# A two-layer attention and mixture-of-experts trunk: attention values of the small heads computed turned and in pairs, from probabilities divided early, and a router that takes its input by feature blocks

## The chip, the cores and the metric

The kernel runs on one core of one Trainium2 chip. The metric is the device time of one execution in microseconds; the time given for a kernel is the median of several runs. All arithmetic on the path is float32.

## The reference, cut to what matters

Two layers, each with a mixing part (three kinds of attention side by side) and a mixture of 32 experts with a router. Sequence 256, width 1024.

```python
for l in range(DEPTH):                              # 2 layers
    z = _rms_norm(x, norm_mix[l]) @ w_in[l]
    ya = _diff_attention(...)                       # "A": 4 heads of 128 value columns
    yb = _dsa_attention(...)                        # "B": 4 heads of 64
    yc = _mla(...)                                  # "C": 4 heads of 64
    mix = jnp.concatenate([ya, yb, yc], axis=-1)
    x = x + mix @ w_out[l]
    x = x + _hier_moe(_rms_norm(x, norm_ffn[l]), ...)
return _rms_norm(x, norm_final)

# in each attention, for 128 queries: p = softmax(logits); out = p @ v
# in _hier_moe: group and expert logits = normed x @ w_group, w_expert; 2 of the 8 experts
# of the best group per token; h = silu(x @ w_gate[e]) * (x @ w_up[e]); y = h @ w_down[e]
```

## The kernel before, in words

The program is written out by hand for each engine, with semaphores between them; each engine runs its own instructions in the order of the code. The 256 tokens lie in two tiles of 128 (`t` = 0, 1). The expert weights (32 experts in each layer, three chunks of 2 MB each: gate, up, down) stream through a ring of eight slots of 2 MB and three further places that hold other tensors during the attention part (two in `arena`, one made of `x` and `bias`). A load is issued by the queue on SP when its slot has been given back (`slot_free`), or when the tensor that lay in its place is no longer read. In the first round of a layer SP issues the chunks in the order `[0..5, 8, 9, 6, 7, 10, 12, 13, 11, 14, ...]`: 8 and 9 wait until the attention's last squares are summed (`ssq_ready`), 6 and 7 until an output matrix's slot is free, 10 for `sums_open` and `x_spent`, and 12 and 13 (`REFILL`) for the first products of expert 0 (`steps_used`). A quarter of chunk 11 goes to `spare`, the upper half of `xT`.

The attention part works through 16 steps (`STEPS`): four of kind C, four of kind B, eight of kind A; the first half of each kind is for tile 0 and the second for tile 1. A step of C or B covers two heads ("maps") side by side. For one step: `logits` (TensorE, two steps per call), `front` (VectorE: scale, bias, and the largest value), `exp` (ScalarE, which also sums the row), `combine` (VectorE: the reciprocal of the sum; for A also the difference of two maps), `turn_p` (TensorE transposes the probabilities), `turned` (ScalarE copies them to SBUF), `values` (TensorE), `finish` (VectorE divides the result by the sum and writes it to `rows`). Projections of the layer's input (`pair`, `columns`, `av_rows`) are put between these steps by hand as work for TensorE.

After the last steps the eight blocks of 128 mixed features of a tile are transposed (`turn_mix`), copied by ScalarE to `xT` (`mixT`) and multiplied by the output matrix (`out_half(t, half, k0, k1)`: blocks k0 to k1 for 512 output columns). `add_half` adds the result to `x`; `squares` and POOL give the RMS factor; `turn_xn` transposes `x` for the router, with a stride of 8 features, and `router(t)` multiplies it by 40 columns. `route` (VectorE) chooses the experts, `place_first` and `gather_first` bring the tokens to their experts, and `products` (at L1738) is the first work on expert weights. The next layer, or the end, follows after 32 experts.

Of the kernel before, what the change touches and what calls it, by code (L numbers as in the profile page):

```python
# [20 lines left out]
ALU = mybir.AluOpType  # L21
# [7 lines left out]
P = 128  # L29
# [54 lines left out]
PJ_EV = 9 + 4 + 2  # L84
# [143 lines left out]
def trunk(nc, x_d, w_in, w_out, norm_mix, norm_ffn, rel_bias, lam_q1, lam_k1, lam_q2, lam_k2,  # L228
          diff_subln, mla_q_norm, mla_kv_norm, w_uq, w_ukv, w_group, b_group, w_expert, b_expert,
          w_gate, w_up, w_down, norm_final, consts_d, onehot_d, flip_d, out_d):  # L230
# [3 lines left out]
    with ctx:  # L234
# [39 lines left out]
        ssq, mean, rms = sb("ssq", 16), sb("mean", 16), sb("rms", 16)  # L274
# [51 lines left out]

        spare = (xT[:, KD // 2:, :].rearrange("p j s -> p (j s)"),)
        h_rows = take(HALF)
        y = take(D_MODEL)
        pick = take(TOK * P).rearrange("p (t s) -> p t s", t=TOK)  # L330
# [66 lines left out]
        xnT_done, xnT_read, xnT_upper = sem("xnT_done"), sem("xnT_read"), sem("xnT_upper")  # L397
# [70 lines left out]
        def load_router(eng, l):  # L468

            loads = (  # L470
                (wr[:, :, 0:N_GROUPS], w_group.rearrange("l (p j) n -> l p j n", j=KD)[l]),
                (wr[:, :, R_EXP:], w_expert.rearrange("l (p j) n -> l p j n", j=KD)[l]),
                (br[:, 0:N_GROUPS], bcast_row(b_group, l, N_GROUPS)),
                (br[:, R_EXP:], bcast_row(b_expert, l, N_EXPERTS)),
            )
# [8 lines left out]
        def _(sp):  # L484
# [8 lines left out]
            for l in range(DEPTH):  # L493
# [24 lines left out]
                for m in range(ROUNDS):  # L518
# [18 lines left out]
                    for c in order_of(m):  # L537
# [49 lines left out]
                        if m == 0 and c == 7:  # L587
                            sp.wait_ge(router_done, at(l, TOK, TOK))
# [10 lines left out]
        def _(pool):  # L599
# [24 lines left out]
            for l in range(DEPTH):  # L624
# [16 lines left out]
                rms_of(own, base, 7, [(15, 16, D_MODEL)])  # L641
# [11 lines left out]
        def _(act):  # L653
# [16 lines left out]
            act.dma_start(gain_R, norm_ffn.rearrange("l (p j) -> p l j", j=KD)).then_inc(gain_r_in, 16)  # L670
# [13 lines left out]
            for l in range(DEPTH):  # L684
# [39 lines left out]
                def turned(s):  # L724
# [3 lines left out]
                    if s >= 2:  # L728
                        act.wait_ge(pv_done, at(l, PV_USES, 3 + s - 1))
                    copy(pT[:, s % 2, 0:n], src[:, 0:n]).then_inc(tr_read, 1)  # L730

                def mixT(t):
                    act.wait_ge(lam_ready, at(l, 2, 2))
                    for half in range(2):
                        if t == 0:
                            src, read = pj_wait(), pj_read
                        else:
                            act.wait_ge(mix_turned, at(l, 2, half + 1))
                            src, read = lg[:, half], mix_read
                        copy(xT[:, 4 * half:4 * half + 4, t * P:(t + 1) * P], src.rearrange("p (j s) -> p j s", j=4),  # L740
                             scale=gsub if half == 0 else 1.0).then_inc(read, 1)
# [62 lines left out]
                for t in range(TOK):  # L804
                    for half in range(TOK - t):
                        act.wait_ge(xnT_done, at(l, 4, 2 * t + half + 1))
                        copy(xT[:, 4 * half:4 * half + 4, t * P:(t + 1) * P],
                             (tr, pj)[t][:, half].rearrange("p (j s) -> p j s", j=4)).then_inc(xnT_read, 1)
# [99 lines left out]
        def _(dve):  # L908
# [11 lines left out]
            for l in range(DEPTH):  # L920
# [140 lines left out]
                def combine(s):  # L1061
# [5 lines left out]
                    if kind == "A":  # L1067
                        own.after()
# [5 lines left out]
                def finish(s):  # L1074

                    kind, i, t = STEPS[s]
                    dve.wait_ge(pv_done, at(l, PV_USES, 3 + s + 1))
                    src = pv[:, (3 + s) % 2, 0:P]
                    if kind == "A":
                        dst = rows[:, t, P * i:P * i + P]  # L1080
                    else:
                        o = {"B": 512, "C": 768}[kind]
                        dst = rows[:, t, o:o + 256].rearrange("p (m h d) -> p h m d", m=2, h=2)[:, i]
                    if kind == "A":
                        v.tensor_scalar(dst, src, rden[:, s % 4, 0:1], None, ALU.mult).then_inc(pv_read, 1)
                        dve.wait_ge(pv_read, at(l, PV_USES, 3 + s + 1))
                        col = 6 + 4 * t + i
                        own.after()
                        own.mark(v.tensor_tensor_reduce(out=sq, in0=dst, in1=dst, scale=1.0, scalar=0.0, op0=ALU.mult,
                                                        op1=ALU.add, accum_out=ssq[:, col:col + 1]))  # L1090
                    else:
                        v.tensor_tensor(dst, src.rearrange("p (m d) -> p m d", m=2),
                                        spread(rden[:, s % 4, :], 2, 64), ALU.mult).then_inc(pv_read, 1)
# [10 lines left out]
                front(2); front(3); combine(2); combine(3); finish(0); finish(1)  # L1104
# [4 lines left out]
                front(4); front(5); combine(4); combine(5); finish(2); finish(3)  # L1109
                front(6); front(7); combine(6); combine(7); finish(4); finish(5)  # L1110
                front(8); front(9); finish(6); finish(7); combine(8); combine(9)
# [11 lines left out]
                finish(14); finish(15)  # L1123
                own.after()
                dve.sem_inc(ssq_ready, 1)
# [20 lines left out]
                def squares(t):  # L1146

                    dve.wait_ge(x_added, at(l, 4, 2 * t + 2))
                    v.tensor_tensor_reduce(out=zT_flat[:, 0:D_MODEL], in0=x[:, t, :], in1=x[:, t, :],
# [794 lines left out]
```

## Time and profile before

| | |
|---|---|
| median of 3 runs | 1207.34 us (1206.68 to 1208.55) |
| the profiled execution | 1206.32 us, of which the profile's span is 1204.5 us |
| TensorE matmul busy (PE) | 1054.3 us, 88% of the span |
| VectorE (DVE) | 344.7 us, 29% |
| ScalarE (ACT) | 235.3 us, 20% |
| GpSimd (POOL) | 18.0 us, 1% |
| DMA | 446.00 MB, mean 370 GB/s |

The profile comes from one execution. Busy time of PE is modelled and includes the flow of data through the array, so that neighbouring matmuls overlap; what one costs is read from the distance between two starts. Each float32 matmul is recorded as two instructions ("x16" is eight matmuls); a transpose of 128x128 is one. PEld is the weight load that goes with a matmul. The span leaves out 1.8 us of the profiled execution.

### The profile page before, as it was taken

How to read it: one execution, taken by the hardware profiler on the slowest of the kernel's cores; microseconds unless marked ns; L12 is line 12 of the kernel's file. 1: busy time of each engine (PE TensorE's matmuls, PEld its weight loads, DVE VectorE, ACT ScalarE, POOL GpSimd, SP SyncE). 2: the span in 40 equal slices, each digit the busy share in tenths (PEclk: the TensorE clock that was granted, in tenths of full speed). 3: DMA queues.
4: the chain of work that ended last, by engine and by line, in shares of the span. 5: the costliest groups of instructions: out<-in, count | busy, mean ns of one | idle time of the engine just before them, and what ended most of it. 6: DMA issues, size and time to landing. Idle time of an engine off the chain costs nothing.

```text
span 1204.5 us, 18674 instructions
## 1 busy us (share of the span) xinstructions
PE 1054.3 (88%) x7889; PEld 594.6 (49%) x7892; DVE 344.7 (29%) x966; ACT 235.3 (20%) x578; POOL 18.0 (1%) x49
## 2 busy tenths in 40 slices
PE   9999999987887888778999999999887968787886
PEld 5777564443434343434468765554443434334433
DVE  3445563211111111111247365622111111111112
ACT  1234311111111111111112441121111111111112
POOL 1000100000000000000010000000000000000000
PEclk9999999998888889888999999999988988898899
DMA  8677579999999999999998056899999999999995
GB/s 303 218 278 280 227 271 429 426 427 426 426 428 424 429 425 427 426 427 427 414 389 309 26 221 254 318 426 428 426 426 426 428 425 427 425 425 427 425 429 214
DMA packets 59142, 446.00 MB, mean 370 GB/s; under 512 B 10888, under 2 KB 15536, under 8 KB 32176
## 3 DMA queue, kind: packets, MB, share of 16 engines
q1 hardware_dynamic: 57216, 443.57, 89.6%
q8 instruction: 65, 1.06, 0.4%
q10 hardware_dynamic: 1840, 1.19, 0.3%
q14 instruction: 21, 0.17, 0.0%
HBM read 442.63 MB, written 2.11 MB: 369 GB/s over the span
## 4 chain that ended last, share of the span: by engine, by line
PE 49%; DMA 44%; SPq 3%; DVE 2%; issue 1%; ACT 1%; POOL 0%; POOLq 0%; ACTq 0%; DVEq 0%
DMA ring<-in_w_up 39%; PE pv L1738 11%; PE pj L1396 8%; PE tr L1757 4%; PE pj L1637 4%; DMA arena<-in_w_up 4%; PE lg L1765 4%; PE pj L1765 3%; SPq L577 3%; PE pj L1402 2%; PE pj L1487 2%; PE tr L1725 1%; PE lg L1426 1%; PE pv L1749 1%; PE pj L1608 1%
## 5 line engine op out<-in xcount | busy, mean ns | idle before, releaser
L1738 PE MATMUL pv<-ring,xT 128*32 128x256 f32 x3136 | 287.7, 446 | 84.5 <-DMA ring<-in_w_up 52.2
L1738 PEld LDWEIGHTS pv<-ring,xT 128*32 128x32 f32 x3136 | 141.9, 123 | 188.2 <-issue 140.7
L1235 DVE TENSOR_SCALAR arena<-arena 128x128 f32<-128x128 f32 x64 | 14.5, 227 | 663.5 <-ACT arena L817 663.2
L1765 PE MATMUL lg<-arena 128*128 128x512 f32 x256 | 131.9, 597 | 0.0
L1765 PE MATMUL pj<-arena 128*128 128x512 f32 x256 | 130.7, 592 | 0.0
L656 ACT ACTIVATE arena<-pv 128x256 f32<-128x256 f32 x64 | 24.5, 383 | 512.2 <-PE pv L1738 512.2
L656 ACT ACTIVATE arena<-tr 128x512 f32<-128x512 f32 (+3 forms) x168 | 92.3, 558 | 125.1 <-PE tr L1757 107.0
L1738 PE MATMUL pv<-arena,xT 128*32 128x256 f32 x640 | 88.5, 434 | 19.6 <-DMA ring<-in_w_up 19.6
L1396 PE MATMUL pj<-xT,ring 128*128 128x256 f32 x448 | 100.6, 381 | 0.0
L1396 PEld LDWEIGHTS pj<-xT,ring 128*128 128x128 f32 x448 | 83.9, 190 | 12.9 <-issue 1.0
L1757 PE MATMUL tr<-ring,arena 128*32 128x512 f32 x696 | 84.2, 594 | 1.9 <-issue 1.9
L1765 PEld LDWEIGHTS pj<-arena 128*128 128x128 f32 x256 | 48.6, 190 | 61.2 <-issue 61.2
L1738 PEld LDWEIGHTS pv<-arena,xT 128*32 128x32 f32 x640 | 42.7, 120 | 47.6 <-issue 34.8
L1765 PEld LDWEIGHTS lg<-arena 128*128 128x128 f32 x256 | 43.6, 190 | 40.7 <-issue 40.7
L1236 DVE RECIPROCAL arena<-arena 128x128 f32<-128x128 f32 x64 | 61.0, 953 | 2.2
L1725 PEld LDWEIGHTS tr<-arena,rows 128*128 128x128 f32 x448 | 55.0, 201 | 10.7 <-issue 10.7
L1725 PE MATMUL tr<-arena,rows 128*128 128x128 f32 x448 | 55.3, 284 | 3.7 <-issue 3.7
L1637 PE MATMUL pj<-ring,xT 128*128 128x512 f32 x128 | 57.9, 598 | 0.0
L1749 PEld LDWEIGHTS pv<-con,arena 128*128 128x128 f32 x128 | 20.2, 207 | 59.7 <-issue 38.6
L1738 PE MATMUL pv<-x,xT 128*32 128x256 f32 x160 | 31.3, 556 | 14.4 <-DMA ring<-in_w_up 14.4
L1749 PE MATMUL pv<-con,arena 128*128 128x128 f32 x128 | 32.4, 335 | 12.1 <-ACT arena L656 12.1
L1757 PEld LDWEIGHTS tr<-ring,arena 128*32 128x32 f32 x696 | 22.5, 109 | 41.3 <-issue 36.5
(226 smaller groups left out, 933.2 us busy)
## 6 DMA issues: line engine op xcount, KB each, us to landing
ring<-in_w_up SPq DMA_DIRECT2D x48, 2048.0 KB, 38.8
ring<-in_w_gate SPq DMA_DIRECT2D x46, 2048.0 KB, 43.6
ring<-in_w_down SPq DMA_DIRECT2D x42, 2048.0 KB, 42.2
arena<-in_w_down SPq DMA_DIRECT2D x14, 2048.0 KB, 42.3
arena<-in_w_gate SPq DMA_DIRECT2D x12, 2048.0 KB, 46.0
ring<-in_w_in SPq DMA_DIRECT2D x10, 2048.0 KB, 20.0
arena<-in_w_up SPq DMA_DIRECT2D x8, 2048.0 KB, 38.1
ring<-in_w_out SPq DMA_DIRECT2D x4, 2048.0 KB, 16.2
```

The costliest lines, as they stand in the source:

```text
L577: sp.dma_start(halves[i], w[:, i * steps:(i + 1) * steps]).then_inc(slot_full[s], 16)
L656: return nc.scalar.activation(out, in_, ACT.Copy, **k)
L1236: own.link(v.reciprocal(sig, sig))
L1396: ins = mm(out, w[:, j], xT[:, j, :], start=(j == 0), stop=(j == KD - 1))
L1402: ins = mm(out, src[:, j, t * P:(t + 1) * P], weights(i, n)[:, j, c:c + m], start=(j == 0), stop=(j == KD - 1))
L1487: ins = mm(bank[:, 0:R5], xT_raw[:, j, t * P:(t + 1) * P], weights(0, n5)[:, j, :], start=(j == 0), stop=(j == KD - 1))
L1637: ins = mm(pj[:, half], xT[:, k, t * P:(t + 1) * P], weights(6 + half)[:, k, :], start=(k == 0), stop=(k == KD - 1))
L1725: ins = mm(wide_ps[:, j * n:(j + 1) * n], rows[:, t, j * P:(j + 1) * P], pick[:, t, 0:n], start=(t == 0), stop=(t == TOK - 1))
L1738: ins = mm(gu_ps[i * CAP:(i + 1) * CAP, :], xg[:, j, c:c + CAP], w, start=(j == 0), stop=(j == KD - 1), tile_position=(0, i * CAP), skip_g ...
L1749: turn_(h_ps[:, c].rearrange("p h s -> p (h s)"), by_step[:, c], ident)
L1757: ins = mm(tr[k * CAP:(k + 1) * CAP, half], hid[:, b, k % 2, k // 2, :], rows_of[k][:, 512 * half:512 * half + 512], start=True, stop=True ...
L1765: ins = mm(acc[t][half], pgT[:, b, t, :], y[:, 512 * half:512 * half + 512], start=False, stop=last, skip_group_check=True)
```

## The change

It has these parts.

* Steps of kind B and C divide early: `combine` now multiplies both maps by the reciprocals, before the transpose. `turn_p` waits for that (`mixed_p`) and no longer for `exp`.
* `values_pair(s)` replaces `values(s)` and `values(s+1)` for B and C: the values (64 columns) are the stationary operand and the turned probabilities (128 columns) the moving one, and the two steps go to the two column halves of the array (`tile_position=(0, 64 * i)`). The result comes out turned, and one copy on VectorE (`finish_pair`) brings it to `mixT_up`, in what was the upper half of `rows`.
* So only the lower four blocks (kind A) are transposed in `turn_mix` and copied in `mixT`. `out_half` is split in `out_upper` (blocks 4 to 7, from `mixT_up`, first) and `out_lower` (blocks 0 to 3).
* VectorE's `finish(14)`, `finish(15)` and the signal after them come after `add_half(0, 1)`.
* The router takes `x` by blocks of 128 features (its weights and the gain are loaded in that order), the upper half (after the upper `add_half`) and the lower half apart; the squares of tile 1 are summed in two halves. A copy on VectorE moves to ScalarE.
* The quarter chunk for `spare` is issued when the last projection is done, after chunk 5, and not after the router.

```diff
                 def turn_p(s):
...
-                    if kind == "A":
-                        pe.wait_ge(mixed_p, at(l, 8, s - 7))
-                    else:
-                        pe.wait_ge(exped, at(l, NS, s + 1))
+                    pe.wait_ge(mixed_p, at(l, NS, s + 1))
...
+                def values_pair(s):
+
+                    kind, _, t = STEPS[s]
+                    pe.wait_ge(tr_read, at(l, TR_EV, 12 + s + 2))
+                    pe.wait_ge(pv_read, at(l, PV_USES, use_of(s) - 1))
+                    n = nk(t)
+                    bank = pv[:, use_of(s) % 2]
+                    vv = bv if kind == "B" else vC
+                    for m in range(2):
+                        for k in range(t + 1):
+                            for i in range(2):
+                                h = i + 2 * m
+                                ins = mm(bank[64 * i:64 * i + 64, m * P:(m + 1) * P], vv[:, k, 64 * h:64 * h + 64],
+                                         pT[:, (s + i) % 2, m * n + k * P:m * n + (k + 1) * P],
+                                         start=(k == 0), stop=(k == t), tile_position=(0, 64 * i), skip_group_check=True)
+                    ins.then_inc(pv_done, 1)
...
                 def combine(s):
...
                     own.mark(v.reciprocal(rden[:, s % 4, :], den[:, s % 2, :]))
-                    if kind == "A":
-                        own.after()
+                    own.after()
+                    if kind != "A":
+                        both = prob[:, s % 2, 0:2 * n].rearrange("p (m k) -> p m k", m=2)
+                        v.tensor_tensor(both, both, spread(rden[:, s % 4, :], 2, n), ALU.mult).then_inc(mixed_p, 1)
+                    else:
...
+                def finish_pair(s):
...
+                    v.tensor_copy(mixT_up[:, t, o:o + 2, :].rearrange("p j s -> p (j s)"), pv[:, use_of(s) % 2, 0:2 * P]
+                                  ).then_inc(pv_read, 1)
...
-                turn_mix(0)
-                out_half(0, 1, 0, KD // 2)
                 turn_p(12); turn_p(13); logits(14)
-                out_half(0, 1, KD // 2)
+                out_lower(0, 1)
                 values(12); values(13)
+                out_upper(0, 0)
                 turn_p(14); turn_p(15); values(14); values(15)
...
-                out_half(1, 1, 0, KD // 2)
-                turn_xn(0)
-                out_half(1, 1, KD // 2)
-                router(0)
-                out_half(1, 0, 0, KD // 2)
+                out_upper(1, 1)
+                turn_mix(1)
+                turn_xn(0, 0)
+                turn_xn(0, 1)
+                out_lower(1, 1)
+                router(0, 0, True)
+                router(0, 1, False)
+                out_upper(1, 0)
...
                 add_half(0, 1)
+                finish(14); finish(15)
+                own.after()
+                dve.sem_inc(ssq_ready, 1)
                 mix_norm(1)
...
-                        if m == 0 and c == 7:
-                            sp.wait_ge(router_done, at(l, TOK, TOK))
+                        if m == 0 and c == 5:
+                            sp.wait_ge(pj_done, at(l, PJ_EV, PJ_EV - 1))
                             sp.dma_start(spare[0], down_v[l * N_EXPERTS + SPLIT // 3][:, 0]).then_inc(spare_full[0], 16)
```

What ScalarE does in this stretch is the same code before and after: `exp(12)`, the copy of the last projection, `mixT(0)` and only then `exp(13)`.

TensorE's instructions from the last three matmuls of `av_rows` to the second part of the first output product, before. L1381 are the transposes of `turn_mix(0)`, L1637 is `out_half`, L1439 `turn_p(12)` and `turn_p(13)`, L1426 `logits(14)`.

```order
L1608 MATMUL pj<-ring,xT 128x512 x3
L1381 MATMUL pj<-con,rows 128x128 x8
L1637 MATMUL pj<-ring,xT 128x512 x4
L1439 MATMUL tr<-con,arena 128x128 x4
L1426 MATMUL lg<-arena 128x256 x4
L1637 MATMUL pj<-ring,xT 128x512 x4
```

The same place in the changed kernel, where L1652 is `out_upper`, L1393 `turn_mix(0)`, L1448 `turn_p`, L1438 `logits(14)` and L1661 `out_lower`.

```order
L1625 MATMUL pj<-ring,xT 128x512 x3
L1652 MATMUL pj<-ring,rows 128x512 x4
L1393 MATMUL pj<-con,rows 128x128 x4
L1448 MATMUL tr<-con,arena 128x128 x4
L1438 MATMUL lg<-arena 128x256 x4
L1661 MATMUL pj<-ring,xT 128x512 x4
```

Four matmuls of the output product stood between `turn_mix(0)` and `turn_p`; they now stand ahead of `turn_mix(0)`, and nothing stands between the two.

VectorE's instructions of steps 6 and 7 (kind B, tile 1) before, from `front(6)` on. L1054, L1058 and L1059 are `front`, L1066 the reciprocals of `combine`, L1092 is `finish` of steps 4 and 5.

```order
L1054 SCALAR_TENSOR_TENSOR arena<-lg,bias 128x512 [waits exped,lg_done]
L1058 TENSOR_TENSOR arena<-arena 128x512 [waits lg_read]
L1059 TENSOR_REDUCE nmax<-arena 128x2 [waits own_dve]
L1054 SCALAR_TENSOR_TENSOR arena<-lg,bias 128x512 [waits exped,lg_done]
L1058 TENSOR_TENSOR arena<-arena 128x512 [waits lg_read]
L1059 TENSOR_REDUCE nmax<-arena 128x2 [waits own_dve]
L1066 RECIPROCAL rden<-den 128x2 [waits exped] x2
L1092 TENSOR_TENSOR rows<-pv,rden 128x2x64 [waits pv_done] x2
```

The same place in the changed kernel; L1076 is the new multiplication of `combine`, L1101 `finish_pair(4)`.

```order
L1060 SCALAR_TENSOR_TENSOR arena<-lg,bias 128x512 [waits exped,lg_done]
L1064 TENSOR_TENSOR arena<-arena 128x512 [waits lg_read]
L1065 TENSOR_REDUCE nmax<-arena 128x2 [waits own_dve]
L1060 SCALAR_TENSOR_TENSOR arena<-lg,bias 128x512 [waits exped,lg_done]
L1064 TENSOR_TENSOR arena<-arena 128x512 [waits lg_read]
L1065 TENSOR_REDUCE nmax<-arena 128x2 [waits own_dve]
L1072 RECIPROCAL rden<-den 128x2 [waits exped]
L1076 TENSOR_TENSOR arena<-arena,rden 128x512 [waits own_dve]
L1072 RECIPROCAL rden<-den 128x2 [waits exped]
L1076 TENSOR_TENSOR arena<-arena,rden 128x512 [waits own_dve]
L1101 COPY rows<-pv 128x256 [waits pv_done]
```

Two multiplications over 512 columns come in between the exponentials and the transposes that wait for them, and two short divisions after the values become one copy.

## Rows read from the trace of the kernel before

**Rows 1.** The page's slices, 40 equal parts of the span: mean busy share of DMA.
```profile
DMA  8677579999999999999998056899999999999995
```

**Rows 2.** Stages of 10 us in layer 1: busy time by engine, granted clock, DMA share, GB/s.
```profile
670.00:680.00 10.00, 10.00 (x37) 5.59 (x36) 2.90 (x6) 4.36 (x14) 0.00 (x0) 1.00 0.00 0
...
780.00:790.00 10.00, 10.00 (x95) 4.54 (x94) 2.84 (x8) 1.81 (x4) 0.00 (x0) 1.00 1.01 429
```

**Rows 3.** Timeline of the SP queue, 730 to 767 us: chunks 8, 6, 7, 12.
```profile
730.68 0.33 SPq L577 DMA_DIRECT2D arena<-in_w_down  x1
...
745.40 0.33 SPq L577 DMA_DIRECT2D ring<-in_w_gate  x1
754.50 0.33 SPq L577 DMA_DIRECT2D ring<-in_w_up  x1
...
766.44 0.33 SPq L559 DMA_DIRECT2D ring<-in_w_gate  x1
```

**Rows 4.** Chain that ended last: the same piece in both layers.
```profile
126.01 3.67 PE pj L1637 x8
...
718.09 3.67 PE pj L1637 x8
```

**Rows 5.** Timeline of PE, layer 1: logits and values of tile 1.
```profile
682.12 0.72 PE L1426 MATMUL lg<-arena 64*128 64x128 f32 x8
682.77 7.17 PE L1396 MATMUL pj<-xT,ring 128*128 128x256 f32 x32
...
699.81 2.00 PE L1457 MATMUL pv<-arena 128*128 128x64 f32 x16
701.65 1.73 PE L1396 MATMUL pj<-xT,ring 128*128 128x256 f32 x7
```

**Rows 6.** Timeline of PE: expert products on four column tiles, and what follows.
```profile
781.32 3.85 PE L1738 MATMUL pv<-ring,xT 128*32 128x256 f32 x64
784.98 1.90 PE L1757 MATMUL tr<-ring,arena 128*32 128x512 f32 x16
```

**Rows 7.** Timeline of all engines, steps 6 and 7, from logits to transposes.
```profile
692.05 1.14 PE L1426 MATMUL lg<-arena 64*128 64x256 f32 x8
...
693.94 0.69 DVE L1058 TENSOR_TENSOR arena<-arena 128x512 f32<-128x512 f32 x1
...
697.31 0.15 DVE L1066 RECIPROCAL rden<-den 128x2 f32<-128x2 f32 x1
...
698.58 0.66 PE L1439 MATMUL tr<-con,arena 128*128 128x128 f32 x4 [0.42 <-ACT arena L719]
```

**Rows 8.** Timeline of all engines around turn_mix(0) in layer 1.
```profile
716.49 0.60 PE L1381 MATMUL pj<-con,rows 128*128 128x128 f32 x4
...
717.43 0.66 PE L1381 MATMUL pj<-con,rows 128*128 128x128 f32 x4 [0.34 <-ACT arena L656]
...
718.12 0.60 ACT L656 ACTIVATE xT<-pj 128x512 f32<-128x512 f32 x1 [0.17 <-PE pj L1381]
718.61 0.50 ACT L719 ACTIVATE arena<-arena,nmax 128x256 f32<-128x256 f32 x1
...
720.18 0.48 DVE L1071 SCALAR_TENSOR_TENSOR arena<-arena,fac 128x256 f32<-128x256 f32 x1
...
721.60 0.60 PE L1439 MATMUL tr<-con,arena 128*128 128x128 f32 x4
```

**Rows 9.** Timeline of all engines, from router(0) to tile 1's ranks.
```profile
745.15 1.88 PE L1661 MATMUL pv<-wr,xT 128*128 128x40 f32 x16
...
755.29 1.23 DVE L1149 CUSTOM_DVE_ANT_0 arena<-x 128x1024 f32<-128x1024 f32 x1
...
757.60 1.11 DVE L1141 SCALAR_TENSOR_TENSOR rows<-x,rms,arena 128x512 f32<-128x512 f32 x1 [0.40 <-POOL rms L620]
...
759.12 0.26 DVE L1156 SCALAR_TENSOR_TENSOR arena<-pv,rms,br 128x40 f32<-128x40 f32 x1 [0.41 <-PE pv L1661]
...
761.60 0.41 PE L1714 MATMUL pv<-arena,con 128*128 128x32 f32 x2
```

More of the change, by code:

```diff
@@ L1180, in _ @@
                 add_half(0, 1)
+                finish(14); finish(15)
+                own.after()
+                dve.sem_inc(ssq_ready, 1)
                 mix_norm(1)
                 add_half(0, 0)
-                squares(0)
+                squares(0).then_inc(ssq_ready, 1)
                 own.mark(rows_half(0, 0))
@@ L1186, in _ @@
                 add_half(1, 1)
+                own.mark(squares(1, 512, D_MODEL))
                 route(0)
@@ L1642, in turn_xn, with out_upper @@
-                def turn_xn(t):
-                    pe.wait_ge(x_added, at(l, 4, 2 * t + 2))
+                def out_upper(t, half):
+                    arrived(6 + half)
+                    if t == 1:
+                        pe.wait_ge(x_added, at(l, 4, 2 - half))
+                    elif half == 1:
+                        pe.wait_ge(pj_read, at(l, PJ_EV, PJ_EV - 2))
+                        pe.wait_ge(pv_read, at(l, PV_USES, 3 + PAIRS))
+                    else:
+                        pe.wait_ge(pj_read, at(l, PJ_EV, PJ_EV))
+                    for k in range(KD // 2, KD):
+                        mm(pj[:, half], mixT_up[:, t, k - KD // 2, :], weights(6 + half)[:, k, :], start=(k == KD // 2), stop=False)
@@ L1654, in router @@
+                    ins.then_inc(xnT_done, 1)
+                def router(t, half, first):
+                    pe.wait_ge(xnT_read, at(l, 4, 2 * t + (1 if first else 2)))
+                    if t == 0 and first:
                         pe.wait_ge(pv_read, at(l, PV_USES, PV_USES))
                         pe.wait_ge(wr_ready, l + 1)
-                    for j in range(KD):
-                        if j == KD // 2 and t == 0:
-                            pe.wait_ge(xnT_read, at(l, 3, 2))
-                        elif j == KD // 2:
-                            pe.wait_ge(xnT_upper, l + 1)
-                        ins = mm(pv[:, t, 0:R_COLS], xT[:, j, t * P:(t + 1) * P], wr[:, j, :],
-                                 start=(j == 0), stop=(j == KD - 1))
@@ L1663, in router @@
-                    ins.then_inc(router_done, 1)
+                    for j in range(4):
+                        src = xnT_up[:, t, j, :] if half == 1 else xT[:, j, t * P:(t + 1) * P]
+                        ins = mm(pv[:, t, 0:R_COLS], src, wr[:, 4 * half + j, :], start=first and j == 0, stop=not first and j == 3)
+                    if not first:
+                        ins.then_inc(router_done, 1)
+                out_upper(0, 1)
                 turn_mix(0)
-                out_half(0, 1, 0, KD // 2)
```

187 lines of the change are left out of this document (86 added, 101 removed).

## The prediction

> **What bounds the kernel now.** I read first the slices of the page [rows 1]. DMA is at nine tenths or more nearly everywhere except in the first six slices and around slices 23 to 26: these are the attention parts of the two layers. The stages show the same at closer range [rows 2]: from 670 to 680 us DMA stands at 0.00 with TensorE busy all the time, because every free place is filled; from 780 to 790 us it runs at 1.01 of its share and 429 GB/s. So the kernel has two regimes. In the expert part the end is set by bytes, and the number of bytes stays the same. In the attention part TensorE sets when the first expert products free slots and chunk 12 can be issued, at 766.44 us [rows 3]. If that moment moves by d, all behind it moves by d. The chain has the same piece in both layers, at 126.01 and 718.09 us, 592.08 us apart [rows 4], so I work one layer out and double it.
>
> What counts is therefore the path of TensorE from about 680 us to the first products, waits included. A saving on VectorE or ScalarE there is worth nothing, unless TensorE waits for it.
>
> **Values in pairs.** Before, the 16 instructions of two steps on tile 1 take 701.65 - 699.81 = 1.84 us [rows 5]; those of tile 0 are half as many, 0.92 us. The new form does not occur in the trace. Its nearest row is the expert product on four column tiles: 64 instructions in 784.98 - 781.32 = 3.66 us, 0.057 us each for 256 moving columns [rows 6]. Two tiles with 128 columns each put the same load on the array per instruction, so 16 cost 0.92 us and 8 cost 0.46 us. Going to another tile shape and back has a price too. The logits use half the rows: 8 instructions of 128 columns would take 8 x 0.107 / 2 = 0.43 us if the halves overlap fully, with 0.107 us as one 128-column instruction (twice the 0.057 of the two-tile case, less the gaps), and the next work begins 682.77 - 682.12 = 0.65 us later [rows 5], so the detour costs 0.22 us. I take 1.14 us for tile 1 and 0.68 us for tile 0, a saving of 0.70 and 0.24 us. The bounds are 0.92 and 0.46 us (detour free), and 1.84 and 0.92 us (no overlap).
>
> The Trainium skill ("TensorEngine Tiling (Array Packing)", Key Properties) says that changing the tiling mode drains the engine; the 0.22 us agree. Its Performance Considerations allow up to twofold for this swap of operands; by that the four pairs would save 2.8 us in a layer, against 1.9 us in my sum.
>
> **The early division.** It puts a reciprocal and a multiplication between `exp` and `turn_p` in eight steps. In most of them a projection runs on TensorE between the two and hides it; its own cost on VectorE, 0.69 us for 512 columns as in the addition over the same shape [rows 7], is then free. Where the cover is gone is steps 6 and 7: TensorE already waits there for ScalarE, 0.42 us before `turn_p(7)` [rows 7]. From the start of `logits(6)` to `turn_p(7)` the chain takes 698.58 - 692.05 = 6.53 us, all of it on VectorE and ScalarE. The division adds the reciprocal (0.15 us [rows 7]), the multiplication (0.69) and about 0.09 for the hand-overs: 0.93 us. `logits(6)` itself comes 0.24 + 0.70 = 0.94 us earlier by the first two pairs. So `turn_p(7)` starts at 698.58 - 0.94 + 0.93 = 698.57 us: what the first two pairs save is spent, and the 0.24 us of the third too, since TensorE only waits longer. What is left is the fourth pair, 0.70 us less some 0.1 us because it waits for both turned steps: 0.6 us earlier from there on.
>
> **The order around `turn_mix(0)`.** This is the part that costs most. ScalarE runs `mixT(0)` ahead of `exp(13)`, and `mixT(0)` waits for the transposes of `turn_mix(0)`. Before, `turn_mix(0)` starts at 716.49 us, the exponentials of step 13 at 718.61, the difference of maps at 720.18 for 0.48 us, and TensorE arrives at `turn_p` at 721.60 [rows 8]: the four matmuls of `out_half` from 718.09 [rows 4] to 721.60, 3.5 us, hide it. Now these 3.5 us stand ahead of `turn_mix(0)`. `out_upper` starts at about 716.4 - 0.6 = 715.8, `turn_mix(0)` at 719.3. ScalarE's copy starts 718.12 - 717.43 = 0.69 us after the transposes do, the exponentials 718.61 - 718.12 = 0.49 us after the copy, and the result is there 720.18 + 0.48 - 718.61 = 2.05 us later [rows 8]: 722.55. TensorE has by then only four transposes and the two of `turn_p(12)` to do, 6 x 0.107 = 0.64 us, and is idle from 719.95 to 722.6: **2.65 us**. Queued behind it are `logits(14)` and with it steps 14 and 15, and the output product. `turn_p(13)` was due at 721.60 + 0.21 = 721.81; it comes 0.8 us later. In that figure the transposes that are no longer made and the copy that TensorE waited for (0.34 us [rows 8]) are already counted.
>
> **From there to the router.** The matmuls are the same but in another order; `turn_mix(1)` has four transposes fewer (0.43 us), and its copy is now waited for a little, 0.1 us. Router(0), before at 745.15 us [rows 9], comes 0.8 - 0.43 + 0.1 = 0.5 us later.
>
> **The router.** After the last `add_half`, the squares of 512 columns take half of 1.23 us [rows 9]; `rows_half`, which starts at 757.60 when the RMS is there, starts 0.6 us earlier, takes 1.11 us, and `route(1)` follows at 758.1 + what came before, where it was at 759.12 because of the router's matmuls [rows 9]. These are half done by then, so VectorE gains about 1.0 us against the old start, 0.5 us of it against TensorE's own arrival after the re-ordering. But TensorE reaches the ranks of tile 1 at 761.60 after its matmuls with hardly any wait, and no matmul has gone. I take 0.2 us as gain. The strided transposes go at the same rate as the others, and the copy that left VectorE lay under POOL's RMS.
>
> **Loads.** Chunks 8 and 9 wait for `finish(15)`, which is now behind `out_upper(0, 0)` (3.5 us) and `add_half(0, 1)`: from 730.68 [rows 3] to about 735.3 us. The two and the half chunk behind them are 5.24 MB, 12.2 us at 429 GB/s [rows 2], and with 1 us to start end at 748.5. Chunk 6 is issued at 745.9, queues and ends at 753.4; chunk 7 comes at 755. So 1.6 us of air remain, and the quarter for `spare` no longer falls in it. I cost this at nothing.
>
> **The sum.** Per layer +0.5 - 0.2 = +0.3 us, twice +0.6 us. The profiled execution of 1206.32 us would become 1206.9 us. It lies 1.02 us below the median of the runs shown, 1207.34 us, which would become **1207.9 us**. A measurement of this kernel can tell about 0.2% (2.4 us) from no change.
>
> **The rivals.**
> *The pairs do not overlap* (slower). Then they cost what the single steps do, `logits(6)` is not earlier, `turn_p(7)` is 0.93 us late, and with the 0.1 us the stretch is 1.03 us later where my sum has it 0.6 us earlier. That is 1.63 us per layer, 3.3 us in all: 1211.2 us. It decides from a cost of about 1.7 us for 16 instructions. Against it stand the four-tile rows [rows 6]; for it, that two tiles with weights of 64 columns occur nowhere. The Trainium skill ("TensorE: Matmul & The Clock Gate", The mechanism) says that a weight load overlaps running matmuls only where the row group differs, and here both tiles use all rows; by that rule this rival would hold. The expert products also use all rows and go at 0.057 us each, so the trace speaks against it. Chance 0.16.
> *The wait behind `turn_mix(0)` is not paid* (faster). If the exponentials of step 13 did not come behind `mixT(0)` on the path, 2.65 us per layer or 5.3 us would be gone: 1202.6 us. It would need the result within 0.65 us of the transposes' start, where the rows give 3.2 us. I keep it, with other savings that I may have missed, at 0.12.
> *The late chunks 8 and 9 bind.* If they come over 1.6 us later than I have it, chunk 7 is pushed back; only beyond the air behind chunk 7 as well would the restart at chunk 12 suffer. With 1 us of that in each layer, 1209.9 us. Chance 0.04.
> *The sum as worked out*: 0.68. Its parts nearly cancel, so its own range is 1205.4 to 1210.2 us, and of the 0.68 some 0.54 fall within 0.2%, 0.06 below and 0.08 above.
>
> **How the numbers follow.** Low end: free detours (0.22 us less on two pairs ahead of `logits(6)` and on the fourth, 0.66 us) and a multiplication at the 0.48 us of VectorE's cheapest two-operand row near it [rows 8], 0.21 us, give -0.87 us per layer, 1206.2 us; with 0.5 us per layer for a shorter wait, 1205.2 us. High end: no overlap, 1211.2 us. I give 1205.0 to 1211.2 us. Faster 0.12 + 0.06 = 0.18; same 0.54; slower 0.16 + 0.04 + 0.08 = 0.28.
>
> **What would show it.** In the changed profile the pairs stand in 64-column tiles, 16 instructions in some 1.1 us. `turn_p(7)` starts 6.5 + 0.9 us after `logits(6)`. Between `turn_mix(0)` and `turn_p(13)` TensorE is idle for some 2.6 us, ended by VectorE. The first products come within 1 us of 765.3 us in layer 1 (plus 0.3 from the layer before). The DMA is full from there to the end as before. The prediction is wrong if a pair costs as much as two single steps, if that idle stretch is missing or longer, or if DMA has a gap between the first products and the end that it had not.

## The result, and the profile after

| | before | after |
|---|---|---|
| median | 1206.25 us (1204.48 to 1209.86, 20 runs) | 1209.94 us (1207.77 to 1218.66, 20 runs) |
| the profiled execution, its span | 1206.32, 1204.5 us | 1210.86, 1209.0 us |
| PE busy | 1054.3 us | 1050.9 us |
| DVE, ACT busy | 344.7, 235.3 us | 351.0, 234.2 us |
| DMA | 446.00 MB, 370 GB/s | 446.00 MB, 369 GB/s |

The ratio is 1.0034 [1.0022, 1.0046]: slower by 3.7 us. TensorE has less to do than before and the bytes are the same, so the time must come from when things happen. I measure a layer from the first values that the change touches (`values` of steps 0 and 1 before, the first `values_pair` after) to the first expert products. In layer 1 this is 680.31 to 765.26 us before, 84.95 us, and 682.79 to 769.69 us after, 86.90 us. Before:
```profile
680.31 1.00 PE L1457 MATMUL pv<-arena 128*128 128x64 f32 x8
...
765.26 3.83 PE L1738 MATMUL pv<-ring,xT 128*32 128x256 f32 x64
```
After:
```profile
769.69 3.88 PE L1764 MATMUL pv<-ring,xT 128*32 128x256 f32 x64
```

The slices of the page, the granted clock and DMA, answer to [rows 1]:
```profile
PEclk9999999998898889889999999999989888898889
DMA  8587489999999999999998065899999999999995
```
The DMA is full in the same slices as before; the first six slices sum to 40 tenths in both, and only share them out otherwise.

The timeline of PE in layer 1, from the first pair on, answers to [rows 5] and [rows 7]:
```profile
682.79 0.66 PE L1463 MATMUL pv<-arena 128*64 128x128 f32 x8
683.38 1.09 PE L1448 MATMUL tr<-con,arena 128*128 128x128 f32 x8
...
693.76 1.13 PE L1438 MATMUL lg<-arena 64*128 64x256 f32 x8
...
699.96 0.66 PE L1448 MATMUL tr<-con,arena 128*128 128x128 f32 x4 [0.83 <-DVE arena L1076]
701.21 0.66 PE L1448 MATMUL tr<-con,arena 128*128 128x128 f32 x4 [0.60 <-DVE arena L1076]
...
702.55 1.09 PE L1463 MATMUL pv<-arena 128*64 128x128 f32 x16
703.58 2.64 PE L1408 MATMUL pj<-xT,ring 128*128 128x256 f32 x11
```
By the starts a pair of tile 0 takes 0.59 us (683.38 - 682.79) and one of tile 1 takes 1.03 us (703.58 - 702.55). TensorE now waits twice for VectorE's multiplication, and `turn_p(7)` starts 7.45 us after `logits(6)`.

The same place as [rows 8], all engines of after in layer 1:
```profile
721.90 0.60 PE L1393 MATMUL pj<-con,rows 128*128 128x128 f32 x4
722.34 0.38 PE L1448 MATMUL tr<-con,arena 128*128 128x128 f32 x2
...
723.18 0.50 ACT L726 ACTIVATE arena<-arena,nmax 128x256 f32<-128x256 f32 x1
...
724.75 0.48 DVE L1080 SCALAR_TENSOR_TENSOR arena<-arena,fac 128x256 f32<-128x256 f32 x1
725.29 0.44 PE L1448 MATMUL tr<-con,arena 128*128 128x128 f32 x2 [2.57 <-DVE arena L1080]
725.66 1.74 PE L1438 MATMUL lg<-arena 64*128 64x256 f32 x8
...
727.33 4.74 PE L1661 MATMUL pj<-ring,xT 128*128 128x512 f32 x8
...
731.90 1.05 PE L1474 MATMUL pv<-arena 128*128 128x128 f32 x8
```
The idle stretch of 2.57 us is there, ended by VectorE. But look at what follows it: `logits(14)` takes 1.67 us from start to start, where the same eight instructions took 1.06 us at 693.76, and the next eight take 4.57 us where they took 3.5 before. The stretches of 1 us say why. The columns are the length, the busy time of PE, PEld, DVE, ACT and POOL with the number of instructions, then the granted clock, the DMA share and GB/s:
```profile
723.00:724.00 1.00, 0.00 (x0) 0.00 (x0) 0.00 (x0) 1.00 (x4) 0.00 (x0) 1.00 1.03 442
...
725.00:726.00 1.00, 0.71 (x6) 0.52 (x8) 0.23 (x1) 0.24 (x1) 0.00 (x0) 1.00 0.79 328
726.00:727.00 1.00, 1.00 (x8) 0.59 (x4) 0.00 (x0) 0.15 (x1) 0.00 (x0) 0.52 0.78 320
727.00:728.00 1.00, 1.00 (x3) 0.50 (x2) 0.58 (x1) 0.00 (x0) 0.00 (x0) 0.50 0.06 25
...
729.00:730.00 1.00, 1.00 (x3) 0.52 (x2) 0.97 (x2) 0.96 (x4) 0.00 (x0) 0.77 0.00 0
730.00:731.00 1.00, 1.00 (x3) 0.38 (x2) 0.93 (x4) 0.82 (x3) 0.00 (x0) 1.00 0.00 0
```
TensorE does nothing from 722.7 to 725.3 us, works again for some 0.7 us at a granted clock of 1.00, and then the clock stands at 0.50 (1.2 instead of 2.4 GHz) until about 729.5 us. I call this a fall. The clock comes back while the engine works. Before, the clock was 1.00 throughout this stretch (718 to 726 us).

The chain that ended last has it in both layers, where [rows 4] had 3.67 us:
```profile
132.08 5.33 PE pj L1661 x8
...
727.40 4.67 PE pj L1661 x8
```

From router(0) to the first products it takes 765.26 - 745.15 = 20.11 us before and 769.69 - 749.93 = 19.76 us after. SP of after issues chunks 8, 6, 7 and 12:
```profile
739.25 0.33 SPq L580 DMA_DIRECT2D arena<-in_w_down  x1
...
750.18 0.33 SPq L580 DMA_DIRECT2D ring<-in_w_gate  x1
759.67 0.33 SPq L580 DMA_DIRECT2D ring<-in_w_up  x1
...
770.88 0.33 SPq L562 DMA_DIRECT2D ring<-in_w_gate  x1
```
Against [rows 3] the last one is 4.44 us later, and the span 4.5 us longer: next to nothing is lost or won behind it. Of the 4.44 us, 2.01 arise in layer 0 (86.96 against 84.95 us from the first values to the products) and 1.95 in layer 1 (86.90); the rest is a start of layer 0 that is 0.16 us earlier, and 0.6 us more between the two stretches.

### The profile page after: what moved, and what is told of

The parts are those of the page before. It is cut to its first block, busy times and chain, and to the rows that moved or that the text cites. A ratio compares the mean times of both kernels' runs of the same rounds, so it can differ in the third digit from the quotient of the medians.

```text
span 1209.0 us, 18644 instructions
## 1 busy us (share of the span) xinstructions
PE 1050.9 (87%) x7873; PEld 591.1 (49%) x7876; DVE 351.0 (29%) x976; ACT 234.2 (19%) x576; POOL 18.3 (2%) x49
## 2 busy tenths in 40 slices
DMA packets 59014, 446.00 MB, mean 369 GB/s; under 512 B 10760, under 2 KB 15408, under 8 KB 32048
## 3 DMA queue, kind: packets, MB, share of 16 engines
q8 instruction: 65, 1.06, 0.4%
## 4 chain that ended last, share of the span: by engine, by line
PE 48%; DMA 45%; SPq 3%; DVE 1%; issue 1%; ACT 1%; POOL 0%; POOLq 0%; ACTq 0%; DVEq 0%
DMA ring<-in_w_up 36%; PE pv L1764 11%; PE pj L1408 7%; PE tr L1783 4%; DMA arena<-in_w_up 4%; DMA ring<-in_w_down 3%; PE lg L1791 3%; SPq L580 3%; PE pj L1791 3%; PE pj L1661 3%; PE pj L1414 2%; PE pj L1652 2%; PE pj L1504 2%; PE tr L1751 2%; PE lg L1438 1%
## 5 line engine op out<-in xcount | busy, mean ns | idle before, releaser
L1764 PEld LDWEIGHTS pv<-ring,xT 128*32 128x32 f32 x3136 | 144.7, 123 | 182.2 <-issue 133.5
L1764 PE MATMUL pv<-arena,xT 128*32 128x256 f32 x640 | 85.4, 422 | 21.7 <-DMA ring<-in_w_up 21.7
L663 ACT ACTIVATE xT<-tr 128x512 f32<-128x512 f32 x34 | 20.3, 596 | 90.7 <-PE tr L1751 89.9
```

Of the source, the lines that this page charges most:

```text
L663: return nc.scalar.activation(out, in_, ACT.Copy, **k)
L1764: ins = mm(gu_ps[i * CAP:(i + 1) * CAP, :], xg[:, j, c:c + CAP], w, start=(j == 0), stop=(j == KD - 1), tile_position=(0, i * CAP), skip_g ...
```

## The experiments

I had two questions: whether the clock, and not a wait that I had overlooked, makes the difference to my sum, and whether each priced part of the sum has the size I gave it. The time of a layer serves better than the whole time, because in the traces the start of the same layer jitters by about 1 us. All kernels below are the changed kernel with one edit, if nothing else is said.

**`exp(13)` ahead of `mixT(0)`.**
```diff
+                exp(13)
                 mixT(0)
-                exp(13); turned(12); turned(13); exp(14); ...
+                turned(12); turned(13); exp(14); ...
```


> The changed kernel with exp(13) ahead of mixT(0) on ScalarE; nothing else. Theory (wait and clock): the idle 2.57 us of TensorE ahead of turn_p(13) and the 1.2 GHz stretch behind it both come from mixT(0) standing before exp(13); without it 2.6 us of wait and some 1.8 us of slow matmuls go in each layer, 8 to 9 us in all: about 1201.5 us, ratio 0.996 to the kernel before, with the granted clock at 1.00 from 718 to 734 us. Rival A (the slow matmuls have another cause, such as loads landing in SBUF or the new place of mixT_up): only the wait goes, 5 us: about 1204.8 us, 0.999, and out_lower(0, 1) still takes 4.7 us and more. Rival B (the restart is bound by the late chunks 8 and 9): no more than 1 us is gained.

Measured: 1201.83 us (1200.59 to 1203.80), ratio to the kernel before 0.9966 [0.9954, 0.9979]. PE of this kernel in layer 1:
```profile
716.86 0.60 PE L1394 MATMUL pj<-con,rows 128*128 128x128 f32 x4
717.30 0.60 PE L1449 MATMUL tr<-con,arena 128*128 128x128 f32 x4
717.83 1.13 PE L1439 MATMUL lg<-arena 64*128 64x256 f32 x8
718.89 3.70 PE L1662 MATMUL pj<-ring,xT 128*128 128x512 f32 x8
```
There is no idle stretch and no fall, each layer takes 82.48 us from the first values to the products, and the kernel is faster than both. Exchanging two entries of ScalarE's queue is enough to remove the wait. This takes away wait and fall together, so it doesn't separate them.

**Ten matmuls on zeros in the idle stretch**, between `turn_p(12)` and `turn_p(13)`. Their result is not read; what is computed stays the same. The `wait_ge` makes sure that the bank that they write to has been read.
```diff
+                turn_p(12)
+                pe.wait_ge(lg_read, at(l, NS, 14))
+                for _ in range(10):
+                    mm(lg[:, 0], zeros[:, 0:P], zeros[:, P:P + 512], start=True, stop=True)
+                turn_p(13); logits(14)
```


> The changed kernel with ten matmuls on zeros (512 bfloat16 columns each, results discarded) between turn_p(12) and turn_p(13): the wait for turn_p(13) stays as long, but TensorE works through most of it. Theory (clock): the wait stays, the clock stays at 1.00, logits(14) takes 1.06 us and out_lower(0, 1) 3.44 us again, 1.8 us less in each layer: about 1206.2 us, ratio 1.000. Rival A (another cause of the slow matmuls): unchanged, 1209.9 us, ratio 1.003, or a little worse.

Measured: 1206.28 us (1204.96 to 1207.95), ratio 1.0000 [0.9991, 1.0009]. PE of this kernel:
```profile
719.21 0.38 PE L1448 MATMUL tr<-con,arena 128*128 128x128 f32 x2
719.43 2.32 PE L1692 MATMUL lg<-zeros 128*128 128x512 bf16 x10
722.17 0.44 PE L1448 MATMUL tr<-con,arena 128*128 128x128 f32 x2 [0.41 <-DVE arena L1080]
722.54 1.13 PE L1438 MATMUL lg<-arena 64*128 64x256 f32 x8
723.60 3.70 PE L1661 MATMUL pj<-ring,xT 128*128 128x512 f32 x8
```
`turn_p(13)` still starts 2.96 us after `turn_p(12)`, as in after (725.29 - 722.34 = 2.95), and all behind it runs at full clock: 85.26 us in layer 1. The wait for VectorE is unchanged; TensorE now works through most of it, the fall is gone in both layers, and so is the loss against the kernel before, as far as it can be measured. The 0.3 us in each layer that remain lie inside the interval.

**Five such matmuls.** The same edit with `range(5)`.

> The changed kernel with five matmuls on zeros between turn_p(12) and turn_p(13) and not ten as in e2: TensorE works some 1.1 us of the wait and is idle for some 1.5 us before turn_p(13). If the clock falls only after the whole idle stretch of 2.57 us, this one keeps it at 1.00 and stands with e2: 1206.3 us, ratio 1.000. If any idle stretch of over 1 us at this place brings the clock down, it stands with the changed kernel: 1209.9 us, ratio 1.003.

Measured: 1207.17 us (1205.45 to 1210.54, 12 runs), ratio 1.0008 [0.9998, 1.0018]. In its profile the idle stretch is 1.49 us, and the clock stays at 1.00; both layers take 85.27 us.
```profile
722.94 0.44 PE L1448 MATMUL tr<-con,arena 128*128 128x128 f32 x2 [1.49 <-DVE arena L1080]
```
It stands with the ten. A rare fall in the runs without a trace isn't ruled out: the slowest took 1210.54 us.

**`turn_mix(0)` ahead of `out_upper(0, 1)`.**
```diff
-                out_upper(0, 1)
                 turn_mix(0)
+                out_upper(0, 1)
```


> The changed kernel with turn_mix(0) ahead of out_upper(0, 1) on TensorE. The four matmuls then cover exp(13) and its difference of maps as they did before the change; TensorE waits for the copy of the last projection instead, some 0.9 us, ahead of turn_mix(0). Theory (wait and clock): 2.57 - 0.9 + 1.8 = 3.5 us less per layer, about 1202.9 us, ratio 0.997. Rival A: 1.7 us less per layer, 1206.5 us, ratio 1.000.

Measured: 1203.05 us (1202.48 to 1205.66), ratio 0.9976 [0.9967, 0.9985]. TensorE waits 0.86 us ahead of `turn_mix(0)`, and 83.53 us pass in each layer, without a fall. The old order on TensorE removes most of the wait as well, but then TensorE waits for ScalarE's copy of the last projection.

**The two tiles of a pair one after the other** instead of in turn.
```diff
-                        for m in range(2):
-                            for k in range(t + 1):
-                                for i in range(2):
+                    for i in range(2):
+                        for m in range(2):
+                            for k in range(t + 1):
```


> The changed kernel with the loops of values_pair turned around, so that one column half of the array gets all its matmuls before the other: the same instructions without alternation. Theory (the saving is the overlap of the two halves): 16 instructions take about 1.9 us and not 1.03, 8 take 0.9 and not 0.59; by the chain through steps 6 and 7 logits(6) comes 1.2 us later and all behind it, and the fourth pair adds 0.8 us: 1.7 to 2.0 us more per layer, about 1213.5 us, ratio 1.006. Rival (the short time comes from the 64-column weights alone): the time does not change, ratio 1.003.

Measured: 1213.05 us (1209.95 to 1214.16, 5 runs), ratio 1.0055 [1.0041, 1.0069]. PE of this kernel in layer 0:
```profile
96.53 1.58 PE L1463 MATMUL pv<-arena 128*64 128x128 f32 x16
98.04 0.66 PE L1448 MATMUL tr<-con,arena 128*128 128x128 f32 x4
...
99.69 0.66 PE L1463 MATMUL pv<-arena 128*64 128x128 f32 x8
100.29 1.99 PE L1408 MATMUL pj<-xT,ring 128*128 128x256 f32 x8
```
The sixteen take 1.51 instead of 1.03 us, the eight of tile 0 the same 0.6 us. The direction is right, but I had expected 1.9 and 0.9 us, and the single instructions of the trace say why it is less. In both orders the instructions on one column half start 0.109 us apart, once the first two are on their way. In turn, all eight of a half run beside the eight of the other. One half after the other, the second half's first starts at 97.03 us, when the first half still has three to start (the last at 97.35 us), so four of each eight still run side by side; and of the eight of tile 0, four on each half, all do. So what saves time is that the two halves run side by side, and changing halves at each instruction lets all of it do so in the long groups. Layer 0, without a fall, is 86.25 us long, 0.98 more than 85.27: twice 0.48 us for its two pairs of tile 1.

**A short division.** `exp(13)` ahead of `mixT(0)` as in the first, and for steps 6 and 7 the multiplication covers one column of each map, so the other probabilities of these steps stay undivided and the values change.
```diff
+                        w = 1 if s in (6, 7) else n
```


> The kernel of e1 (exp(13) ahead of mixT(0)) in which the early multiplication of steps 6 and 7 covers one column of each map and not 256; all other steps divide in full, so in these two steps (heads of kind B on tile 1) the output is left undivided. Theory (the division stands on the path there, one multiplication of 0.69 us behind exp(7)): turn_p(7) starts 0.5 us earlier and all behind it, 1.0 us less in two layers: about 1200.8 us, ratio 0.9957 (e1: 0.9966). Rival (the wait is that for the exponentials alone, the multiplication lies beside it): no change against e1.

Measured: 1228.22 us, ratio 1.0186 [1.0167, 1.0204], and 81.94 us from the first values to the products, against 82.48. The 0.54 us in a layer are as expected, the whole time is not: the altered values change which experts the tokens go to, and the trace has one more 2 MB load into the ring of each of `in_w_gate`, `in_w_up` (49 for 48) and `in_w_down`: 452.29 for 446.00 MB. At 429 GB/s that is 14.7 us of the 26.4 us that this kernel is slower than the first edit; the rest I did not follow. Only the stretch counts here. In it the wait ahead of `turn_p(6)` falls from 0.83 to 0.30 us.

**Both waits filled.** `exp(13)` moved as in the first, and 3 of the 8 matmuls of a projection taken from behind `turn_p(7)` to ahead of `turn_p(6)`.
```diff
+                map_upper(0, 3)
                 turn_p(6); turn_p(7)
                 logits(8); values_pair(6)
-                columns(map_bank[:, SEQ:2 * SEQ], weights(4)[:, :, 3 * P:4 * P]).then_inc(pj_done, 1)
+                map_upper(3, KD).then_inc(pj_done, 1)
```


> The kernel of e1, with three of the eight matmuls of the last B and A projection (the second half of map_bank) moved ahead of turn_p(6), into the waits for the early division (0.83 and 0.60 us ahead of turn_p(6) and turn_p(7)). Theory (TensorE is the path, and these waits are the price of the early division): 1.3 us of work goes into 1.43 us of waits, logits(8) starts no later, and 2.4 us go in two layers: about 1199.4 us, ratio 0.9946. Rival A (late chunks 8 and 9, or DMA, now bind the restart): less than 1 us is gained over e1. Rival B (moving them delays the chain of steps 8 and 9): no gain.

Measured: 1198.94 us (1198.43 to 1201.34, 5 runs), ratio 0.9945 [0.9928, 0.9962], the fastest version of this study. PE of this kernel:
```profile
693.08 1.46 PE L1620 MATMUL pj<-xT,ring 128*128 128x256 f32 x6
694.37 0.60 PE L1449 MATMUL tr<-con,arena 128*128 128x128 f32 x4
695.32 0.66 PE L1449 MATMUL tr<-con,arena 128*128 128x128 f32 x4 [0.35 <-DVE arena L1077]
```
Of 1.43 us of waiting 0.35 is left. A layer takes 81.30 us (81.32 in layer 1), 1.17 less than with the first edit alone.

**The changed kernel again**, three times without an edit, one execution each, because the fall need not come every time.

> The changed kernel once more, unaltered, for its profile. The theory of the clock says that TensorE idles 2.57 us ahead of turn_p(13) in both layers; whether the clock then falls differs from one execution to another (it fell in three of four such stretches so far): each layer either shows out_lower(0, 1) at over 4.6 us with a granted clock near 0.5, or at 3.5 us with 1.00. The span follows: 1209 us with two falls, some 2 us less for each one missing.

> The changed kernel once more, unaltered, for its profile: whether the clock falls behind the idle 2.57 us in each layer (two falls: 1209 us of span; none: 1205 us; the stretch from values_pair(0) to products(0) is 85.3 us without a fall and 86.9 us with one).

> As e10: the changed kernel unaltered, one more profile, to see in how many of the executions the clock falls, by the stretch from values_pair(0) to products(0): 85.3 us without a fall and 86.9 us with one.

Measured: 1206.73, 1210.27 and 1209.52 us. In the first the clock never falls, with the same idle stretch:
```profile
722.95 0.44 PE L1448 MATMUL tr<-con,arena 128*128 128x128 f32 x2 [2.57 <-DVE arena L1080]
723.31 1.14 PE L1438 MATMUL lg<-arena 64*128 64x256 f32 x8
724.38 3.70 PE L1661 MATMUL pj<-ring,xT 128*128 128x512 f32 x8
```
Both its layers take 85.27 us. The second falls in both (86.90 and 86.85 us). The third has no fall in layer 0 (85.26 us) and a longer one in layer 1 (88.36 us):
```profile
722.75 0.69 PE L1448 MATMUL tr<-con,arena 128*128 128x128 f32 x2 [2.57 <-DVE arena L1080]
723.37 2.08 PE L1438 MATMUL lg<-arena 64*128 64x256 f32 x8
725.38 5.60 PE L1661 MATMUL pj<-ring,xT 128*128 128x512 f32 x8
```

**A wait in the kernel before.** 20 copies of three columns on ScalarE between `mixT(0)` and `exp(13)`, in the kernel before, to have the idle stretch without the change.
```diff
                 mixT(0)
+                for n in range(20):
+                    copy(scrap[:, 3 * n:3 * n + 3], zeros[:, P:P + 3])
                 exp(13); ...
```


> The kernel before, with twenty copies of three columns (to a tensor that nobody reads) on ScalarE between mixT(0) and exp(13). Each takes about 0.2 us, some of it overlapped, so exp(13) comes 2 to 4 us later; 1.1 us of that was air, and TensorE is idle some 1 to 3 us ahead of turn_p(13), with nothing else of the change in the kernel. Theory (an idle stretch of about 2.5 us at this place makes the clock fall in part of the executions, 1.65 us each): the time rises by twice the idle stretch, and by up to 3.3 us more; runs spread by more than those of the kernel before, and where the profile shows a fall, out_half(0, 1)'s second part takes over 4.6 us. Rival (the fall needs the changed kernel's other work, such as 64-column tiles): the time rises by twice the idle stretch alone, and the clock stays at 1.00 in both layers.

Measured: 1207.89 us (1206.30 to 1210.68, 12 runs), ratio 1.0015 [1.0005, 1.0025]. The copies took only 1.99 us together, TensorE was idle for 0.62 us, the clock stayed at 1.00. This missed the length it was made for and decides nothing on the fall; it costs 0.81 us in each layer.

**The same with 40 copies**, of one column each.

> The kernel before with 40 copies of one column of zeros (instead of the 20 of three columns that e9_idle_in_before had) on ScalarE ahead of exp(13). There the 20 took 1.99 us and left TensorE idle for 0.62 us ahead of turn_p(13); 40 take some 4.0 us, so the idle stretch is to be 2.6 us, the length that it has in the changed kernel, with nothing else of the change. Theory (an idle stretch of this length, and nothing else of the change, lets the granted clock fall): in at least one of the two layers logits(14) and the out_half behind turn_p(13) run at a granted clock near 0.50, logits(14) takes 1.7 instead of 1.1 us, and that layer's stretch is some 1.6 us longer than the other's would be; without a fall the stretch is 0.81 + 2.0 = 2.8 us longer than before in each layer, so the run takes 1206.3 + 5.6 = 1211.9 us without a fall and up to 1215.2 us with two; by the rate of 6 in 10 seen in kernels with the change's stretch, two layers without any fall have a chance of 0.16. Rival (the fall comes from something else in the changed code, the mix of tile shapes or the order of the matmuls): the clock stays at 1.00 in both layers and the time is 1211.9 us, with as narrow a scatter as the kernel before has.

Measured: 1213.34 us (1211.03 to 1217.79, 6 runs), ratio 1.0058 [1.0045, 1.0071]; the profiled execution is the one of 1217.79 us. Its PE in layer 0, and stretches of 1 us there:
```profile
131.96 0.69 PE L1442 MATMUL tr<-con,arena 128*128 128x128 f32 x2 [2.46 <-DVE arena L1074]
132.58 2.08 PE L1429 MATMUL lg<-arena 64*128 64x256 f32 x8
```
```profile
131.00:132.00 1.00, 0.04 (x1) 0.04 (x1) 0.83 (x3) 0.20 (x1) 0.00 (x0) 0.85 0.12 49
132.00:133.00 1.00, 1.00 (x4) 0.67 (x6) 0.00 (x0) 0.32 (x1) 0.00 (x0) 0.50 0.00 0
...
138.00:139.00 1.00, 1.00 (x3) 0.52 (x2) 0.65 (x3) 0.54 (x3) 0.00 (x0) 0.74 0.00 0
```
The clock falls in both layers of a kernel that has nothing of the change but an idle stretch of nearly the same length: `logits(14)` takes 2.0 us in layer 0 and 1.85 in layer 1. Without a fall a layer would take 84.95 + 0.81 + (3.83 - 1.99) = 87.60 us, with 3.83 us as the 40 copies together; it takes 178.40 - 87.83 = 90.57 and 776.83 - 687.75 = 89.08 us, so the falls cost 2.97 and 1.48 us. The rival, that tile shapes or the new order bring the clock down, is refuted: the fall comes without them.

## Why the prediction was right or wrong

The forecast was 1207.9 us, within 0.2% of before; the time is 1209.94 us, inside the range, but slower by more than that. Part of this closeness is luck: the forecast started from the median of three runs, 1207.34 us, and twenty runs have 1206.25 us. As a change, 0.6 us was forecast and 3.7 us came. The sum holds for what it counts and leaves one thing out.

**What held.** Without a fall the change costs 85.27 - 84.95 = 0.32 us in a layer, where my sum said 0.3. That it agrees this well is luck too, because errors in the terms cancel. In the execution without a fall router(0) comes 0.66 us later than before, counted from the first values (65.50 against 64.84 us; I had 0.5), and the router gives back 0.34 us (I had 0.2). The pairs take 0.59 and 1.03 us (0.68 and 1.14 predicted), but what stands around them became slower by some 0.2 us, so `logits(6)` is 0.77 us earlier and not 0.94. I had also put the two old pairs of tile 0 at 0.92 us each, as half of 1.84; by the starts they take 0.84 and 0.94 us; and I worked out `out_upper` from 716.4 us, where [rows 8] have 716.49. `turn_p(7)` comes 7.45 us behind `logits(6)`; 6.53 + 0.93 = 7.46 was predicted. The idle stretch is 2.57 us, not 2.65. The short division shows that one multiplication lies on the path with its whole length: over one column of each map it takes 0.16 instead of 0.69 us, and the stretch is 0.54 us shorter. One sign of the forecast was missed: the first products come at 769.69 us and not within 1 us of 765.6; in the execution without a fall they come at 765.71 us.

**The step that failed** is "This is the part that costs most": I priced the 2.65 us of idle time behind `turn_mix(0)` as a wait and nothing more, so that `turn_p(13)` "comes 0.8 us later" and "the matmuls are the same" behind it. They are the same in number and not in time. The clock may be at half behind such a stretch, and a fall costs 1.58 to 1.69 us in four of the five layers of the changed kernel that show one, and 3.09 us in the fifth (86.96, 86.90, 86.90, 86.85 and 88.36 against 85.27 us). That the fall and not the wait makes the loss is shown by the matmuls on zeros: same wait, no fall, 85.26 us and a ratio of 1.0000. That the stretch alone brings it is shown by the kernel before with 40 copies.

**How it adds up.** The four profiled executions of after have five falls in eight layers, 1.92 us each on average. By that a run costs 2 x 0.32 + 2 x 5/8 x 1.92 = 3.0 us more than before; measured are 3.7 us, with an interval of 2.7 to 5.5 us. Eight layers are few for a rate, so this is an estimate. It may also account for the wider scatter of after, but those runs have no trace. The slowest of them, 1218.66 us, is another matter: its granted clock over the whole execution is 0.899, where the other nineteen have 0.934 to 0.943, and two falls of this kind would not lower it so far. What it lost I can't say.

**The rivals.** *The pairs do not overlap* didn't come true: 0.064 us for each of 16 instructions, where the old form had 0.115. With the two halves one after the other sixteen cost 1.51 us, but half of them still overlap there, so no run shows what a pair without any overlap costs. The Trainium skill ("TensorE: Matmul & The Clock Gate", The mechanism) ties the overlap of a weight load with running matmuls to different row groups; here both tiles use all rows and still run side by side, 1.03 against 1.51 us, so here the measurement goes against the rival that I had drawn from that rule. *The wait behind `turn_mix(0)` is not paid* didn't either, but pointed at the right place: the version without wait and fall gains 2.79 us in a layer over the 85.27 us of the changed kernel without a fall, where I had given 2.65, and stands at 0.9966. *The late chunks 8 and 9* did no harm: chunk 8 is issued at 739.25 us where I had 735.3. Of the 4 us, 2.5 were there at the first values of the layer already and 1.6 come with the fall, and chunks 6 and 7 are shifted with it (750.18 and 759.67 us); without a fall chunk 8 is issued at 735.26 us. In the trace of after the DMA works without a gap from 740 us to about 758.2 us and then stands still until chunk 7, so some 1.5 us of air are left, where I had 1.6; and the last issue moves to within 0.1 us of what the span does.

## What to carry to other kernels

A wait on TensorE can cost more than its length: where a change opens an idle stretch on TensorE, read the granted clock of the next microseconds, and price the work behind it at half speed as a second case with its own chance. When work is moved on one engine, look at every queue that is in a fixed order with respect to it; here one `exp` behind the copy of `mixT(0)` on ScalarE decided between 0.34% slower and 0.34% faster. And a form that makes TensorE quicker gives nothing where the next wait is on VectorE: here the saving became idle time at `turn_p(6)` and `turn_p(7)` until other matmuls were put there.

## What the runs showed of the hardware

- The same idle stretch does not always bring the clock down. In twelve layers with 2.46 or 2.57 us of idle time (the changed kernel, the one with one tile after the other, and the kernel before with 40 copies) it fell in eight; with 0.41, 0.62 or 1.49 us it fell in none of the two layers of each. At a rate of eight in twelve, two layers without a fall have a chance of one in nine, so these two alone don't show that 1.49 us are safe. Two executions of the same kernel differ in it, and the two layers of one. The Trainium skill ("TensorE: Matmul & The Clock Gate", What's actually happening) says that the chip's watch on activity runs freely and isn't tied to the kernel's start; that layers of one kernel differ fits it, but no run shows the cause.
- The fall can begin behind the idle stretch: in layer 1 of after the clock is 1.00 in the stretch and for the first 0.7 us of work, and at 0.50 only then. With 40 copies it began near the end of the stretch in layer 0 and lasted some 7 us, and that fall cost 2.97 us.
- Two tiles of 128 rows by 64 columns, fed in turn, take 0.064 us for each instruction of 128 columns in a group of sixteen; fed one after the other 0.094 us, because then only half of them run side by side. In a group of eight both orders take 0.59 to 0.60 us.
